# A 128x128 block-triangular inverse: its level of 32x32 blocks computed block by block instead of with full-width products and a mask

## What is computed

```python
m = jnp.where(strict, jnp.einsum('bhnid,bhnjd->bhnij', k_beta, k) * decay, 0.0)
a_mat = m + jnp.eye(C, dtype=jnp.float32)
...
sol = lax.linalg.triangular_solve(a_mat, rhs, left_side=True, lower=True, unit_diagonal=True)
```

## Time and profile before

| | |
|---|---|
| three runs | 1144.62, 1144.62, 1147.76 us; median 1144.62 |
| the profiled execution | 1147.81 us; its span 1146.0 us |
| mean granted PE clock | 0.993 |
| PE busy | 1121.3 us, 98% of the span |
| PE weight loads busy | 1043.6 us, 91% |
| DVE, ACT, POOL busy | 559.1 (49%), 567.2 (49%), 678.3 (59%) us |
| the three lines of the big products | 78% of the chain that ended last |
| HBM | 159 GB/s over the span |

### The profile page before, as it was taken

One profiled execution on the slowest core, in us unless ns is written; L12 is line 12 of the kernel. 1 busy time (PEld: TensorE's weight loads), 2 busy tenths in 40 slices (PEclk: granted clock), 3 DMA queues, 4 the chain that ended last, 5 costly groups with the idle time before them and its releaser, 6 DMA issues.

```text
span 1146.0 us, 19832 instructions
## 1 busy us (share of the span) xinstructions
PE 1121.3 (98%) x8108; PEld 1043.6 (91%) x8112; DVE 559.1 (49%) x1042; ACT 567.2 (49%) x894; POOL 678.3 (59%) x355
## 2 busy tenths in 40 slices
PE   8899999999999899999998999999999999999997
PEld 6899999998798799999998999999988978999997
DVE  5678566445412543534545856683634235211333
ACT  7445764434554534444463467543445545444443
POOL 4776567617684347754586658575187634576433
PEclk9899999999999999999998999999999999999999
DMA  7344334524543545555553444455155344555553
GB/s 280 130 165 148 131 133 161 176 65 151 203 149 127 178 170 184 184 185 185 185 177 134 148 143 153 123 176 161 40 199 185 129 149 160 188 184 184 184 183 112
DMA packets 63338, 183.41 MB, mean 160 GB/s; under 512 B 18576, under 2 KB 19088, under 8 KB 63248
## 3 DMA queue, kind: packets, MB, share of 16 engines
q1 hardware_dynamic: 47936, 172.51, 42.9%
q10 hardware_dynamic: 15312, 9.64, 3.1%
HBM read 179.51 MB, written 2.62 MB: 159 GB/s over the span
## 4 chain that ended last, share of the span: by engine, by line
PE 92%; DMA 2%; DVE 2%; ACT 1%; POOL 1%; issue 1%; SPq 0%; DVEq 0%; POOLq 0%; ACTq 0%
PE psum L476 26%; PE psum L477 26%; PE psum L478 26%; DMA sb_raw<-weights 2%; PE psum L613 1%; PE psum L904 1%; PE psum L883 1%; PE psum L657 1%; PE psum L640 1%; PE psum L550 1%; PE psum L789 1%; PE psum L796 1%; PE psum L624 1%; PE psum L750 1%; PE psum L741 1%
## 5 line engine op out<-in xcount | busy, mean ns | idle before, releaser
L379 POOL TENSOR_TENSOR sb_low<-sb_raw,sb_high 128x1024 fp32r<-128x1024 f32 x261 | 627.7, 2416 | 355.3 <-ACT sb_high L369 347.0
L369 ACT ACTIVATE sb_high<-sb_raw 128x1024 fp32r<-128x1024 f32 x322 | 340.4, 1061 | 468.0 <-DMA sb_raw<-weights 406.6
L476 PE MATMUL psum<-sb_h_high,sb_high 128*128 128x256 f32 x1664 | 472.0, 284 | 1.3 <-DVE sb_low L379 1.3
L478 PE MATMUL psum<-sb_h_high,sb_low 128*128 128x256 f32 x1664 | 469.7, 282 | 0.0
L477 PE MATMUL psum<-sb_h_low,sb_high 128*128 128x256 f32 x1664 | 469.3, 282 | 0.0
L476 PEld LDWEIGHTS psum<-sb_h_high,sb_high 128*128 128x128 f32 x1664 | 314.4, 189 | 3.7 <-issue 2.2
L477 PEld LDWEIGHTS psum<-sb_h_low,sb_high 128*128 128x128 f32 x1664 | 313.3, 188 | 0.9
L478 PEld LDWEIGHTS psum<-sb_h_high,sb_low 128*128 128x128 f32 x1664 | 312.6, 188 | 0.0
L379 DVE TENSOR_TENSOR sb_low<-sb_raw,sb_high 128x1024 fp32r<-128x1024 f32 x61 | 94.2, 1557 | 30.0 <-ACT sb_high L369 29.5
L1926 DVE SCALAR_TENSOR_TENSOR sb_sq<-sb_th,psum 128x512 f32<-128x512 f32 x22 | 15.1, 688 | 140.3 <-ACT sb_th L1360 140.3
L1697 DVE SCALAR_TENSOR_TENSOR sb_conv<-psum,sb_param,sb_conv 128x255 f32<-128x255 f32 (+1 forms) x144 | 58.3, 474 | 48.6 <-ACT sb_conv L1172 48.5
(11 more groups left out here) (278 smaller groups left out, 1594.0 us busy)
## 6 DMA issues: line engine op xcount, KB each, us to landing
sb_raw<-weights SPq DMA_DIRECT2D x322, 512.0 KB, 3.2
sb_pre_gain<-pre_gains ACTq DMA_DIRECT2D x6, 512.0 KB, 5.1
sb_post_gain<-post_gains ACTq DMA_DIRECT2D x6, 512.0 KB, 3.7
sb_kx<-mem SPq DMA_DIRECT2D x2, 512.0 KB, 4.3
sb_x<-x SPq DMA_DIRECT2D x1, 1024.0 KB, 11.2
t_dram<-sb_sq ACTq DMA_DIRECT2D x4, 256.0 KB, 2.9
out<-sb_x SPq DMA_DIRECT2D x4, 256.0 KB, 2.1
m_dram<-sb_m ACTq DMA_DIRECT2D x8, 64.0 KB, 2.0
```

The source lines that it names most:

```text
L369: nc.scalar.activation(high[:, n % HIGHS, :], raw[:, n % RAWS, :], ACT.Copy).then_inc(high_ready, 1)
L379: eng.tensor_tensor(low[:, k, :], raw[:, k, :], high[:, n % HIGHS, :].bitcast(F32), ALU.subtract).then_inc(low_ready[k], 1)
L476: pe.matmul(out, a[0], b[0], start=start, stop=False, **kw)
L478: return pe.matmul(out, a[1], b[0], start=False, stop=stop, **kw)
```

## The change

Level 32 of the inverse is computed with the 32x32 blocks alone. Each matrix has two pairs; p = 0 has its first block on rows 0 to 31 and its second on 32 to 63, p = 1 on 64 to 95 and 96 to 127. The groups g are taken in two halves hf (g 0 and 1, then 2 and 3), and one PSUM bank holds a half's 16 products of 32x32 (8 matrices, two pairs on different partitions).

- First product: weights `m_up[first rows, second columns]`, 32x32, moving `t_low[first rows, first columns]`, 32 columns, written to the partitions of the second block. p alternates from matmul to matmul.
- DVE copies each pair's result (32 partitions x 256) to `prod` on the second block's rows. The mask, its constant and the helper `even` are gone.
- Second product: weights `t_up[second, second]`, moving `prod[second]`, written to the second block's partitions. DVE writes minus the result to `t_low`; nothing is subtracted, since that block of `t_low` is zero.
- Only the new block of `t_low` is transposed, 32x32, one bank for each p and half, and ACT copies 32 partitions x 256 of it to `t_up`.
- The transposes of a half are followed at once by level 64's first product for its two groups, where all the transposes came before all of those products.

```diff
-                for g in range(4):
-
-                    what = ("mt", 32, g)
-                    o = claim(what, (dve_gdn, what))
-                    for i in range(4):
-                        mm = pe.matmul(o[:, i * 64:(i + 1) * 64], m_up[:, g, i, :], even(t_low[:, g, i:i + 1, :], 32), start=True, stop=True)
-                    mm.then_inc(pe_gdn.sem, mark(pe_gdn, what))
+                def by_pair(what, reader, act):
+
+                    o = claim(what, reader)
+                    for n in range(8):
+                        g, i = 2 * what[2] + n // 4, n % 4
+                        for p in range(2):
+                            last_one = act(o, n, g, i, 2 * BLOCK * p, 2 * BLOCK * p + BLOCK)
+                    last_one.then_inc(pe_gdn.sem, mark(pe_gdn, what))
+
+                def at_rows(t, row, g, i, col):
+                    return t[row:row + BLOCK, g, i, col:col + BLOCK]
+
+                for hf in range(2):
+                    by_pair(("mt", 32, hf), (dve_gdn, ("mt", 32, hf)), lambda o, n, g, i, first, second: pe.matmul(
+                        o[second:second + BLOCK, n * BLOCK:(n + 1) * BLOCK], at_rows(m_up, first, g, i, second), at_rows(t_low, first, g, i, first), start=True, stop=True))
                 pe.wait_ge(up_loaded, 16 * BLOCKS * (layer + 1))
...
+                for hf in range(2):
+                    pe.wait_ge(*dve_gdn.at(layer, ("mt", 32, hf)))
+                    by_pair(("tmt", 32, hf), (dve_gdn, ("t_low", 32, hf)), lambda o, n, g, i, first, second: pe.matmul(
+                        o[second:second + BLOCK, n * BLOCK:(n + 1) * BLOCK], at_rows(t_up, second, g, i, second), at_rows(prod, second, g, i, 0), start=True, stop=True))
+                for hf in range(2):
+                    pe.wait_ge(*dve_gdn.at(layer, ("t_low", 32, hf)))
+                    for p in range(2):
+                        what = ("t_up", 32, hf, p)
+                        o = claim(what, (act_gdn, what))
+                        for n in range(8):
+                            g, i, first = 2 * hf + n // 4, n % 4, 2 * BLOCK * p
+                            second = first + BLOCK
+                            tr = pe.transpose(o[0:BLOCK, n * BLOCK:(n + 1) * BLOCK], at_rows(t_low, second, g, i, first), ident[second:second + BLOCK, second:second + BLOCK])
+                        tr.then_inc(pe_gdn.sem, mark(pe_gdn, what))
+                    for g in (2 * hf, 2 * hf + 1):
+                        what = ("mt", 64, g)
...
-                    pe.wait_ge(*act_gdn.at(layer, ("t_up", 32, g)))
+                    pe.wait_ge(*act_gdn.at(layer, ("t_up", 32, g // 2, 1)))
...
-                for g in range(4):
-                    copy(flat(t_up[:, g, :, :]), bank(("t_up", 32, g)), pe_gdn, ("t_up", 32, g), act_gdn, ("t_up", 32, g))
+                for hf in range(2):
+                    for p in range(2):
+                        what, first = ("t_up", 32, hf, p), 2 * BLOCK * p
+                        copy(t_up[first:first + BLOCK, 2 * hf:2 * hf + 2, :, first + BLOCK:first + 2 * BLOCK],
+                             bank(what)[0:BLOCK, 0:256].rearrange("p (g h n) -> p g h n", g=2, h=4), pe_gdn, what, act_gdn, what)
...
-                    V.tensor_tensor(prod[:, g, :, :], bank(("mt", 32, g))[:, 0:256].rearrange("p (h n) -> p h n", h=4),
-                                    heads(level_mask, 4), ALU.mult).then_inc(dve_gdn.sem, dve_gdn.mark(("mt", 32, g)))
...
+                blocks = lambda what, rows: bank(what)[rows, 0:256].rearrange("p (g h n) -> p g h n", g=2, h=4)
+                for hf in range(2):
+                    low_parts(ahead(("mt", 32, hf), 2))
+                    dve.wait_ge(*pe_gdn.at(layer, ("mt", 32, hf)))
+                    for second in (BLOCK, 3 * BLOCK):
+                        rows = slice(second, second + BLOCK)
+                        V.tensor_copy(prod[rows, 2 * hf:2 * hf + 2, :, 0:BLOCK], blocks(("mt", 32, hf), rows))\
+                            .then_inc(dve_gdn.sem, dve_gdn.mark(("mt", 32, hf) if second > BLOCK else ("mt_first", hf)))
+                for hf in range(2):
+                    low_parts(ahead(("tmt", 32, hf), 2))
+                    dve.wait_ge(*pe_gdn.at(layer, ("tmt", 32, hf)))
+                    for second in (BLOCK, 3 * BLOCK):
+                        rows = slice(second, second + BLOCK)
+                        V.tensor_scalar(t_low[rows, 2 * hf:2 * hf + 2, :, second - BLOCK:second], blocks(("tmt", 32, hf), rows), -1.0, None, ALU.mult)\
+                            .then_inc(dve_gdn.sem, dve_gdn.mark(("t_low", 32, hf) if second > BLOCK else ("t_low_first", hf)))
```

More of the change, by code:

```diff
@@ L77 @@
 N_FIRST = C_NEGHALF + 16
-C_AFTER, C_UPTO, C_IDXBIAS, C_LEVEL = (N_FIRST + n * P for n in range(4))
-N_CONST = C_LEVEL + 64
+C_AFTER, C_UPTO, C_IDXBIAS = (N_FIRST + n * P for n in range(3))
+N_CONST = C_IDXBIAS + P
 R_CONV, R_MEM, R_GDN, R_DT, R_ALOG = 0, 96, 104, 105, 113
@@ L204, in program @@
         one = const_t[:, C_ONE:C_ONE + 1]
-        level_mask = const_t[:, C_LEVEL:C_LEVEL + 64]
         eps_col = const_t[:, C_EPS:C_EPS + 1]
@@ L356, in heads @@
             return ap.unsqueeze(1).broadcast_to([P, m, ap.shape[-1]])
-        def even(t, s):
-            return t.rearrange("p h (b w c) -> p (h b) w c", w=2, c=s)[:, :, 0, :]
         def highs(act, done, upto):
@@ new lines, in _ @@
+                for hf in range(2):
[14 more added lines that the diff above has]
+                        what = ("mt", 64, g)
+                        o = claim(what, (dve_gdn, what))
+                        for i in range(4):
+                            mm = pe.matmul(o[64:P, i * 64:(i + 1) * 64], m_up[0:64, g, i, 64:P], t_low[0:64, g, i, 0:64], start=True, stop=True)
+                        mm.then_inc(pe_gdn.sem, mark(pe_gdn, what))
@@ L1816, in _ @@
                     by_head(k_dec[:, 4 * g:4 * g + 4, :], ("k_tok", g), k_scale0[:, 4 * g:4 * g + 4], ("k_tok", g))
-                for g in range(4):
-                    low_parts(ahead(("mt", 32, g), 2))
-                    dve.wait_ge(*pe_gdn.at(layer, ("mt", 32, g)))
-                    V.tensor_tensor(prod[:, g, :, :], bank(("mt", 32, g))[:, 0:256].rearrange("p (h n) -> p h n", h=4),
-                                    heads(level_mask, 4), ALU.mult).then_inc(dve_gdn.sem, dve_gdn.mark(("mt", 32, g)))
[L1823 to L1828, removed]
+                blocks = lambda what, rows: bank(what)[rows, 0:256].rearrange("p (g h n) -> p g h n", g=2, h=4)
[13 more added lines that the diff above has]
+                            .then_inc(dve_gdn.sem, dve_gdn.mark(("t_low", 32, hf) if second > BLOCK else ("t_low_first", hf)))
                 for g in range(4):
@@ L1962, in constants @@
     c[:, C_IDXBIAS:C_IDXBIAS + P] = np.where(i[None, :] > i[:, None], NEG, 0.0)
-    k = np.concatenate([np.arange(2 * BLOCK * b, 2 * BLOCK * b + BLOCK) for b in range(BLOCKS // 2)])
-    c[:, C_LEVEL:C_LEVEL + 64] = i[:, None] // BLOCK == k[None, :] // BLOCK + 1
     for col, sgn, d in ((C_INV_A, C_SGN_A, DH), (C_INV_I, C_SGN_I, IDX_DIM)):
```

## The result

The change made the kernel slower: 1151.87 us (median of 14 runs, 1147.93 to 1154.15) against 1145.72 (14 runs, 1143.39 to 1148.2), ratio 1.0052 with a 95% interval of 1.0041 to 1.0063. The forecast was 1138 and faster.

The account below looks back on a forecast made before the run. PE was taken to bound the kernel, busy 98% of the span and pacing the inverse itself. Saving 3.3 us in each of two layers, 6.7 in all, took the median of 1144.62 to 1137.9, rounded 1138; range 1134.5 to 1147.

Parts of the forecast that it names:

- rival B: PE's clock falls during the 32x32 passes, 3.4 us lost per fall; one per layer gives 1144.7 us; chance 0.08.
- this end of the range (1137.0): Level 32 passes at 16 ns, alternating row halves side by side: chain 0.45 us a layer shorter, bounded by DVE.
- The pacing of the stretch by PE: In the inverse, 13.74 us a layer, PE paces itself; DVE and ACT wait for PE.
- the hand-overs of DVE and PE: Level 32: DVE hands to PE in 0.07 us; a reader starts 0.03 to 0.05 after a matmul's end.
- the covered work of ACT: ACT's copies and mem_high products lie beside PE in the inverse, with 0.6 us to spare.
- the loads and the bank waits: The t_up load, the constants load and changed bank rotation were each put at nothing.
- The 31 ns of a pass in one tile: Level 32: a 32-column pass takes 31 ns, from the line through 112 ns at 128 columns and 58 at 64.
- The forecast's sum: Over both layers' inverses, 2 x 3.3 = 6.7 us less than before.
- A: Passes get no shorter below 64 columns (58 ns): 0.4 us a layer worse, 1145.3 us; chance 0.18 with cases between.
- C: Alternating tiles writing one PSUM bank wait for each other, 0.22 us a pass: 41 us over both layers, 1186; chance 0.12.

Follow-up runs that it names:

- fill_narrow: The changed kernel with 30, 8 and 12 f32 matmuls of 32x32 put where PE waits for DVE; 1149.47 us, ratio 1.0032 to the kernel before.
- full_transposes: The change for the two products alone, with the transposes 128x128 again and all before level 64's first product; 1143.32 us, ratio 0.9977 to the kernel before.
- fill_later: The changed kernel with 1 and 2 wide matmuls in the later gaps only, the first gap left empty; 1154.26 us, ratio 1.0072 to the kernel before.
- late_wide: The changed kernel with six wide bf16 matmuls before the second half's transposes, no gap filled; 1155.49 us, ratio 1.0082 to the kernel before.
- fill_wide: The changed kernel with seven wide bf16 matmuls, results unread, put where PE waits for DVE; 1139.47 us, ratio 0.9949 to the kernel before.
- fill_wide_in_turn: The changed kernel with seven wide fillers and one pair's products after the other's instead of alternating; 1151.94 us, ratio 1.0047 to the kernel before.
- before_one_wait: The kernel before, with every group of the second product waiting for DVE's last copy of the first; 1157.18 us, ratio 1.0093.
- fill_first: The changed kernel with 4 wide bf16 matmuls in the first gap only, before the second product; 1145.08 us, ratio 0.9989 to the kernel before.

## Why the prediction was wrong

**The step that failed is the clock, which the sum put at nothing.** Every pass of the chain was priced at a granted clock of 1.00. The runs showed 0.50 for 13.7 and 13.6 us of the two layers. The prediction had this as rival B, and got both its chance and its price wrong.

The chance of 0.08 rested on two arguments. One was that 4.7 us of 64x64 passes had run at 1.00. That is true and says little, since those passes came behind 9 us of full ones. The other was that "PE has no idle gap above 0.2 us in my chain". It failed because two tiles side by side start a pass every 16 ns, not every 31: the first product was over at 1.1 instead of 2.0, and the gap before the second is 1.0 us. The prediction had worked out this end of the range (1137.0) and didn't look at the gap that it opens. Nor would a chain without gaps have been safe: in layer 1 of fill_narrow there was none, and the clock fell.

The price, "One such fall per layer cancels the gain: 1144.7", took 6.8 us at half rate from the earlier trace rows. In the change a fall lasted twice that. The length isn't a constant: over the stretches of the profiled executions above it was from 3.4 us (full_transposes) to 17.1 (fill_later, late_wide), and no run shows what sets it.

**The sum with the clock in it.** A mean clock c over the span means 2 x (1 - c) x span at half rate, and half of that lost. Before: 0.004 x 1145 = 4.6 us lost; the change: 0.016 x 1150 = 18.4. The difference is 13.8. The work itself, as fill_wide shows from the first k_tok load to the solves, is 14.62 - 11.06 = 3.56 us a layer shorter, 7.1 in all. 13.8 - 7.1 = 6.7 slower; measured 6.15. So near an agreement is partly luck. The sum takes half of every fall as lost, and in the profiled execution it was less: from L727's first load to the streamed products the change took 29.4 and 29.7 us, fill_wide 24.0 in both layers, so falls of 13.7 us cost 5.4 and 5.7, not 6.8. And runs of the change with the same mean clock of 0.985 lie from 1147.94 to 1151.59 us. The sum is good to some 3 us, and within that nothing else is needed for the loss. That the clock is the cause is shown by fill_wide, which differs in the fillers alone.

**What was right.** The pacing of the stretch by PE, the hand-overs of DVE and PE (second product at 2.11 against 2.16, transposes of layer 1 at 3.90, with 16 ns passes 3.86 by the same chain), the covered work of ACT, the loads and the bank waits: none of them shows up. The 31 ns of a pass in one tile was right too (fill_wide_in_turn). The forecast's sum was 6.7 us; with the clock held, fill_wide has 6.3, fillers and all.

**The rivals.** A (no shorter pass than 58 ns) is refuted by 31 ns in one tile and 16 in two. The rule of the Trainium skill (TensorE: Matmul & The Clock Gate, LDWEIGHTS), columns over 1.2 GHz, gives 27 ns for 32 columns; within one tile these passes stand 31 apart, so the trace is some 5 ns above it. The some 60 cycles per matmul of the Trainium skill (TensorEngine Tiling (Array Packing), Instruction Overhead), by estimate 25 ns at 2.4 GHz, lie under the 31 of one tile and can't bind across tiles: two tiles in turn start every 16 ns. C (alternating tiles wait for each other in one bank) is refuted by the same 16 ns into one bank, on different partitions.

**The range** went to 1147 to take in A and B. With two falls of 13.7 us at half of their length each, B's price would have been 1137.9 + 13.7 = 1151.6, still just under the 1151.87 measured.

## What to carry to other kernels

Making the passes of a stretch cheaper turns PE-paced work into waits for DVE, and the clock, not the passes, can then set the time. Before making matmuls narrow, read how long the stretch will be without wide work, gaps included, and put wide work that is needed anyway (or, failing that, useless wide matmuls) into the gaps. Then look at the granted clock in more than one stretch and at the spread of the runs, since the same instructions kept it in one layer and lost it in the other. Don't price a fall of the clock by the length that another one had: here they lasted from 3.4 to 17.1 us.

## What the runs showed of the hardware that had not been expected

- One gap of 0.6 us between wide f32 passes with 64 moving columns was followed by a fall of 10.2 us in one layer and by none in the other (before_one_wait), by the same instructions. Such chances show in the spread: fill_first ran from 1139 to 1150 us, and in most kernels the runs with the lower mean clock tend to be the slower.
- 32x32 f32 passes start 31 ns apart in one tile, and 16 ns apart on average when they alternate between row halves, into one PSUM bank. Sixteen 32x32 f32 transposes, eight on one quarter and eight on another, take (0.54 - 0.19)/15 = 0.023 us each in fill_wide, again with the two tiles overlapping where the quarter changes; within the last five, on one quarter, they stand (0.30 - 0.19)/4, about 0.03, apart.
- The fall at the start of layer 0, which has its like near 611 in the earlier trace rows, isn't in every execution: the profiled one of the change had a clock of 1.00 from 45 to 56 us, that of before 0.69. PE's first products behind it (L586, formerly L591) start at 59.6 against 62.4 us, 2.8 us of difference between the two pages. Of the twelve profiled executions ten have this fall, for 3.4 or 6.8 us; those of the change and of fill_narrow don't.
